# Attention outputs scaled before w_out, one bank for both halves, and a new order of residual and splits at two seams

## What is computed

```python
h = h + 0.5 * rms_norm(f, ffn1_post_g)                       # the residual stream called h3 below
z = rms_norm(h, mix_pre_g) @ w_in                            # "in2"
q_na, k_na, v_na, c_q, c_kv, k_rope = jnp.split(z, split_at, axis=-1)
o_na = neighbourhood_attention(...)                          # 8 heads of 64
o_mla = latent_attention(...)                                # 8 heads of 64
mixed = concatenate([rms_norm(o_na, na_out_norm_g),
                     rms_norm(o_mla, mla_out_norm_g)], -1) @ w_out
h = h + rms_norm(mixed, mix_post_g)                          # the residual stream called h4 below
f = swiglu(rms_norm(h, ffn2_pre_g), ffn2_w_gu, ffn2_w_down)
h = h + 0.5 * rms_norm(f, ffn2_post_g)
```

## Time and profile before

| | us |
|---|---|
| median of 3 runs | 998.67 |
| lowest and highest | 997.17 and 1002.05 |
| the profiled execution | 994.14 |
| its span (first to last instruction) | 992.4 |

### The profile page before, as it was taken

The page is one execution under the profiler, slowest core; times in us unless marked ns, Lnnn a source line. Parts: engine busy times, 40 slices in busy tenths (PEclk is TensorE's granted clock), DMA queues, the critical chain, the costliest instruction groups (busy, mean ns, idle before and its releaser), DMA issues.

```text
span 992.4 us, 13886 instructions
## 1 busy us (share of the span) xinstructions
PE 952.9 (96%) x4548; PEld 786.9 (79%) x4548; DVE 502.7 (51%) x841; ACT 491.2 (49%) x771; POOL 337.3 (34%) x170
## 2 busy tenths in 40 slices
PE   8998979999999999999999999998999989999997
PEld 6876867888878888888878888887878868888886
DVE  5439596554544434343564434337488674334332
ACT  5353935654455454444544454436436464444442
POOL 2410000102434444344444444553512034343442
PEclk9999999999999999999999999999999999999999
DMA  7844454354655566778566566655612246665562
GB/s 232 282 131 147 144 173 141 109 153 142 204 161 181 174 190 190 239 225 242 175 183 190 171 192 188 188 157 161 190 43 86 85 147 194 192 187 175 190 190 81
DMA packets 132768, 169.29 MB, mean 171 GB/s; under 512 B 16707, under 2 KB 88430, under 8 KB 132598
## 3 DMA queue, kind: packets, MB, share of 16 engines
q1 hardware_dynamic: 132566, 168.67, 55.1%
q10 hardware_dynamic: 160, 0.07, 0.0%
HBM read 167.61 MB, written 1.10 MB: 170 GB/s over the span
## 4 chain that ended last, share of the span: by engine, by line
PE 79%; DVE 11%; ACT 5%; issue 3%; DMA 0%; POOL 0%; DVEq 0%; POOLq 0%; ACTq 0%; SPq 0%
PE acc L786 24%; PE acc L788 24%; PE acc L787 24%; PE tp L831 4%; DVE w_lo L1173 4%; ACT w_hi L462 1%; PE sc L916 1%; PE acc L1108 1%; DVE u L1261 1%; ACT junk L468 1%; DVE xt_lo L1556 1%; DVE u L1225 0%; DVE u L1321 0%; DVE h L1546 0%; PE tp L936 0%
## 5 line engine op out<-in xcount | busy, mean ns | idle before, releaser
L462 ACT ACTIVATE w_hi<-w_raw 128x1024 fp32r<-128x1024 f32 x305 | 322.0, 1060 | 376.2 <-PE acc L788 346.0
L1770 POOL TENSOR_TENSOR w_lo<-w_raw,w_hi 128x1024 fp32r<-128x1024 f32 x124 | 302.5, 2440 | 397.0 <-ACT w_hi L462 396.9
L1173 DVE TENSOR_TENSOR w_lo<-w_raw,w_hi 128x1024 fp32r<-128x1024 f32 x181 | 234.8, 1306 | 330.6 <-ACT w_hi L462 328.9
L786 PE MATMUL acc<-w_hi,xt_hi 128*128 128x512 f32 (+1 forms) x880 | 350.0, 398 | 9.5 <-DVE w_lo L1173 6.6
L788 PE MATMUL acc<-w_lo,xt_hi 128*128 128x512 f32 (+1 forms) x880 | 342.9, 390 | 0.0
L787 PE MATMUL acc<-w_hi,xt_lo 128*128 128x512 f32 (+1 forms) x880 | 342.2, 389 | 0.0
L786 PEld LDWEIGHTS acc<-w_hi,xt_hi 128*128 128x128 f32 x880 | 165.3, 188 | 46.6 <-DVE w_lo L1173 9.7
L788 PEld LDWEIGHTS acc<-w_lo,xt_hi 128*128 128x128 f32 x880 | 165.1, 188 | 34.7
L787 PEld LDWEIGHTS acc<-w_hi,xt_lo 128*128 128x128 f32 x880 | 165.5, 188 | 32.0
L786 PE MATMUL acc<-w_hi,hid_hi 128*128 128x512 f32 x264 | 103.2, 391 | 0.0
L788 PE MATMUL acc<-w_lo,hid_hi 128*128 128x512 f32 x264 | 102.8, 389 | 0.0
(11 more groups left out here) (198 smaller groups left out, 781.7 us busy)
## 6 DMA issues: line engine op xcount, KB each, us to landing
w_raw<-in_ffn_w_gu SPq DMA_DIRECT2D x176, 256.0 KB
w_raw<-in_w_in SPq DMA_DIRECT2D x68, 512.0 KB
w_raw<-in_w_ffn_in SPq DMA_DIRECT2D x88, 256.0 KB
w_raw<-in_ffn_w_down SPq DMA_DIRECT2D x44, 512.0 KB
w_raw<-in_w_ffn_out SPq DMA_DIRECT2D x22, 512.0 KB
w_raw<-in_w_rnn_out SPq DMA_DIRECT2D x8, 512.0 KB
w_raw<-in_w_attn_out SPq DMA_DIRECT2D x8, 512.0 KB
w_raw<-in_w_o SPq DMA_DIRECT2D x8, 512.0 KB
```

The costliest lines, as they stand in the source:

```text
L462: act.activation(w_hi[:, b, :], w_raw[:, b, :], ACT.Copy).then_inc(hi_done[b], 1)
L786: pe.matmul(o, hi[:, k, rows], wh, start=first and n == 0, stop=False)
L1173: dve.tensor_tensor(w_lo[:, b, :], w_raw[:, b, :], w_hi[:, b, :].bitcast(F32), ALU.subtract).then_inc(lo_done[b], 1)
L1770: pool.tensor_tensor(w_lo[:, b, :], w_raw[:, b, :], w_hi[:, b, :].bitcast(F32), ALU.subtract).then_inc(lo_done[b], 1)
```

## The change

It has two parts.

1. **w_out.** The outputs of both attentions are now multiplied by their row factors in SBUF (`scale_values`, two instructions of 128x512 on VectorE for each attention) before they are transposed, so that na's and mla's products can be summed in one bank. The groups "top" and "bot" become one pair, "out2"; the drains of top and the adding of bot are gone, and the seam reads the bank directly, as at h3 (`post_squares`, `gained`). To have na's factor in time, its squares move from n = 10 to n = 9 on ScalarE, its mean from n = 12 to n = 10 on VectorE, the scaling stands at n = 11, and the turns move from n = 10 and 11 to n = 12 and 13. GpSimd takes na's power before its second slab of w_out. The turns of mla's output move from after the first slab to after the third.
2. **The seams h3 and h4.** On VectorE the residual is added before the two slabs' low parts are written, and of these one is written before each half of `xt_lo`. On ScalarE the squares of tile 1 stand between the two halves of the split of tile 0.

The core of the diff:

```diff
-MQK_AT, ONA_AT = 4, 10
+MQK_AT, ONA_AT = 4, 12
...
             post_squares("f2", 1, G["f2o"] + 1, S["f2o"] + 21, (0,))
             feed(S["in2"], 2)
-            split_new("h3", 0, mix2_g)
+            split_new("h3", 0, mix2_g, (0,))
             post_squares("f2", 1, G["f2o"] + 1, S["f2o"] + 21, (1,))
+            split_new("h3", 0, mix2_g, (1,))
             feed(S["in2"] + 2, 2)
...
-                if n == ONA_AT:
+                if n == 9:
                     for m in range(MT):
                         wait_drained(act, G["na"], m)
                         square("na", 0, m, o2[:, 0, m, :])
...
+            for c in range(2):
+                post_squares("mix", c, G["out2"] + c, S["out2"] + 5 + 2 * c, (0,))
+            feed(S["f3i"], 2)
+            split_new("h4", 0, f3_g, (0,))
+            for c in range(2):
+                post_squares("mix", c, G["out2"] + c, S["out2"] + 5 + 2 * c, (1,))
+            split_new("h4", 0, f3_g, (1,))
+            feed(S["f3i"] + 2, 2)
+            squares_new("h4", 0)
+            split_new("h4", 1, f3_g)
             squares_new("h4", 1)
...
+            def out2_products(half, c, q, ms=range(MT)):
+
+                s, g = S["out2"] + 4 * half + 2 * c + q, G["out2"] + c
+                wait(pe, lo_done[s % RING], s // RING + 1)
+                slab_products(s, [(0, 4 * half + 2 * q), (1, 4 * half + 2 * q + 1)], XT, W,
+                              acc[g % 2 * 2:g % 2 * 2 + 2], half == 0 and q == 0, half == 1 and q == 1, ms=ms,
+                              done=(acc0_full[g % 2], slab_used[s % RING]))
...
+            last = (S["f2o"] + 10, S["f2o"] + 21)
+            finish("f2", 0, G["f2o"], 1, last, h_new)
+            feed(S["in2"], 1)
+            split_new("h3", 0, mix2_g, (0,))
+            feed(S["in2"] + 1, 1)
+            split_new("h3", 0, mix2_g, (1,))
+            finish("f2", 1, G["f2o"], 1, last, h_new)
+            feed(S["in2"] + 2, 1)
+            split_new("h3", 1, mix2_g, (0,))
+            feed(S["in2"] + 3, 1)
+            split_new("h3", 1, mix2_g, (1,))
...
+            def scale_values(name, which, done):
+
+                dve.wait_ge(rs_done, NTH[name])
+                for m in range(MT):
+                    dve.tensor_scalar(o2[:, which, m, :], o2[:, which, m, :], rs[:, ST[name], m:m + 1], None,
+                                      ALU.mult).then_inc(done, 1)
...
-                if n == ONA_AT + 2:
+                if n == 10:
                     mean_square("na")
+                if n == 11:
+                    scale_values("na", 0, na_scaled)
             drain_values2(1, G["mla"])
+            mean_square("mla")
+            scale_values("mla", 1, mla_scaled)
```

More of the change, by code:

```diff
@@ L678, in _, with split_new @@
             mix2_g = par[:, PAR["mix2_g"]:PAR["mix2_g"] + KT]
-            def split_new(name, m, gain):
-                for half in range(2):
+            def split_new(name, m, gain, halves=range(2)):
+                for half in halves:
                     x = X[name] + 2 * m + half
@@ L747, in _ @@
                 square("mla", 0, m, o2[:, 1, m, :])
+            feed(S["out2"] + 4, 2)
             for k in range(2):
                 split(X["omla"] + k, (4 + 2 * k, 5 + 2 * k), par[:, PAR["mla_g"] - 4:PAR["mla_g"] + 4], xt_hi)
-            feed(S["out2"] + 4, 4)
+            feed(S["out2"] + 6, 2)
             f3_g = par[:, PAR["f3_g"]:PAR["f3_g"] + KT]
[L752 to L762, removed]
+            for c in range(2):
[8 more added lines that the diff above has]
+            split_new("h4", 1, f3_g)
             squares_new("h4", 1)
@@ L1141, in _ @@
                 for c in range(2):
[L1142 to L1143 removed]
                     for q in range(2):
[L1145 to L1146 removed]
                         ready(q)
[L1148 to L1149 removed]
+                        out2_products(1, c, q, (m,))
                         if (m, c, q) == (1, 1, 0):
@@ L1565, in _, with finish @@
             mix2_g = pcol("mix2_g")
-            for m in range(MT):
-                mean_square("f2", m)
-                gained("f2", G["f2o"] + 1, 1, 1, S["f2o"] + 21, (m,))
-                feed(S["in2"] + 2 * m, 2)
-                for g in (G["f2o"], G["f2o"] + 1):
-                    wait_drained(dve, g, m)
-                add_normed("f2", m, h_new, lambda m, c: f[:, m, c * W:(c + 1) * W])
-                split_new("h3", m, mix2_g)
+            def finish(name, m, g, row, last_slabs, done):
+                mean_square(name, m)
+                gained(name, g + 1, 1, row, last_slabs[1], (m,))
+                for c in range(2):
+                    wait_drained(dve, g + c, m)
+                add_normed(name, m, done, lambda m, c: f[:, m, c * W:(c + 1) * W])
+            last = (S["f2o"] + 10, S["f2o"] + 21)
[9 more added lines that the diff above has]
+            split_new("h3", 1, mix2_g, (1,))
             mean_square("h3")
@@ new lines, in _ @@
+            last = (S["out2"] + 5, S["out2"] + 7)
+            gained("mix", G["out2"], 0, 2, last[0], (0,))
+            finish("mix", 0, G["out2"], 2, last, h_new)
+            feed(S["f3i"], 1)
+            split_new("h4", 0, f3_g, (0,))
+            feed(S["f3i"] + 1, 1)
+            split_new("h4", 0, f3_g, (1,))
+            gained("mix", G["out2"], 0, 2, last[0], (1,))
+            finish("mix", 1, G["out2"], 2, last, h_new)
+            feed(S["f3i"] + 2, 1)
+            split_new("h4", 1, f3_g, (0,))
@@ L1745, in statistics3 @@
+            feed(S["f3i"] + 3, 1)
+            split_new("h4", 1, f3_g, (1,))
             def statistics3():
```

57 lines of the change are left out of this document (15 added, 42 removed).

## The result

The changed kernel takes **1016.80 us** (1015.82 to 1017.53, four runs) against 998.94 us for the kernel before; the ratio of the runs is 1.018, with a 95% interval of 1.0162 to 1.0197. The forecast had the sign right and the size wrong: +9.5 us and a range up to 1013, where +17.9 was measured. The profiled execution took 1016.76 us (span 1014.9), the profiled one of before 994.14 (span 992.4).

What follows compares the result with a forecast made beforehand. TensorE bounds the touched stretches, so losses pass on in full. h3 +3.2, attention +3.3, h4 +3.0 and w_out 0 give +9.5 us: 1003.6 profiled, 1008.2 us median, range 1003 to 1013.

Steps and rivals of the forecast that it cites:

- The h3 seam: At h3, first product 2.0 us earlier, but TensorE waits for the third and fourth slabs' low parts: +3.2 us.
- The h4 seam: At h4, same shape as at h3, low parts late, tile 1's turn at 17.2 to 17.6 us: +3.0 us.
- The attention: Squares of na at head 9 and turns at heads 12 and 13: 0.6 + 2.5 + 0.2 = +3.3 us.
- Head 10's exponentials: On ScalarE in the attention, they start at 757.3 instead of 753.84, behind the wait for the drained banks.
- Head 12's turn: On TensorE in the attention, it comes at 762.6 against 762.03, part of the delay made up: +0.6 us.
- the two turns: Turns of na, now at heads 12 and 13, cost 3.2 us, of which 0.7 already fell behind head 12: +2.5.
- Scaling: Two new VectorE instructions of 128x512 for na, 0.3 to 0.6 us each; TensorE's turn of na waits for both.
- The GpSimd collision at head 13: GpSimd's second low part, about 761.8 to 764.2, overlaps VectorE's `nm` of head 13; with the scaling +0.2 us.
- w_out: In w_out, three slabs cover the wait of mla's turns for squares, power and scaling: cost nothing.
- The sum: Both seams and the attention: 3.2 + 3.3 + 3.0 = +9.5 us, median 1008.2; chance 0.65.
- rival C: Clock falls to 1.2 GHz in TensorE's seam idle times: h3 3.3 more, h4 3.8; 1011.5 or 1015.3; chance 0.17.

Runs made afterwards that it cites:

- experiment 8: Changed kernel with two low parts earlier on VectorE at each seam, and na's squares behind head 10's exponentials with mean, scaling and turns one head later: 994.68 us.
- experiment 6: Changed kernel with na's squares on ScalarE behind head 10's exponentials, and mean, scaling and turns one head later: 1010.00 us.
- experiment 5: Changed kernel with useless identity products filling TensorE's five longest waits, 14 and 12 at each seam, 11 at head 10: 1005.46 us.
- Experiment 1: The kernel before, run again unchanged to see each run's clock: 998.05 us, ratio 0.9993.

## Why the prediction was right in its steps and wrong in its size

**The h3 seam.** Counted from the first turn, the forecast had the first product at 3.0, the third at 9.5, tile 1's turn at 10.7, the fourth at 14.9 and tile 1's products at 16.0. With the waits filled and the clock at 1.00 these are 3.0, 9.0, 10.2, 14.3 and 15.6, and the stretch costs +2.6 for +3.2. After, with the clock low, tile 1's products come at 18.0, and more is lost behind them: +6.7. The order and its chain were right, the price of the waits 0.6 high.

**The h4 seam.** Third product at 10.3 to 10.6 forecast, 9.6 measured; tile 1 at 17.2 to 17.6, 16.7 with the waits filled. +3.0 forecast, +2.3 at full clock, +4.8 in the run.

**The attention.** Head 10's exponentials were forecast for 757.3 on the clock of before. They come at 766.85, and all up to there stands 9.76 later, so 757.1. Head 12's turn was forecast for 762.6; with the waits filled it comes at 767.17, less 4.68 of delay, 762.5. Behind it come +2.5, as forecast for the two turns, and the whole is +3.0 for +3.3. What the forecast didn't say is what this price stands for. In experiment 8, whose attention is that of experiment 6, head 13's turn comes 2.3 us earlier than before, since the two turns are gone from heads 10 and 11; they then cost 3.1 us from there on, and +0.8 is left. In the changed kernel ScalarE's stand uses up that lead. So the turns cost what I had put on them, but 2.2 of the 3.0 us come back once the squares stand at head 10 and the turns one head later.

**Scaling.** The two instructions start 0.40 us apart, between my ends of 0.3 and 0.6, where VectorE's 1024 elements of a low part take 1.13 from one to the next. That is less than half of it (0.57), so the rule of the Trainium skill, "VectorE: DVE Perf Modes", section "Mode 2×_2P", is borne out in direction; the 0.3 us estimated by it was 0.1 too low. The GpSimd collision at head 13 did not come in the profile of after, where both engines were late by different amounts. With the waits filled it came where it was forecast: GpSimd's low part runs from 766.09 to 768.44, VectorE's `nm` of head 13 starts in it at 767.26 and takes 1.21 us instead of 0.17, and TensorE's first turn of na waits 0.96 us for the scaled output. All of this lies within the +2.5.

**w_out**: forecast 0, measured 0.0, and no idle time at mla's turns.

**The step that failed is the clock.** The sum reckoned every wait at its length alone and put the lower level behind it at nothing. The waits that I summed to +9.5 measured +7.6 to +7.9 (experiment 5 against the runs and the profile of before). The other 10.2 of the 17.9 us are the lower level, which I had put aside as rival C with a chance of 0.17. In C itself two things were off. First, I counted C for the two seams alone (3.3 and 3.8; the filled run gives 4.1 and 2.4). I had written down that head 10's exponentials come 3.4 us late and that TensorE's turn of head 10 is queued behind them, but then asked only when head 12's turn would come, +0.6. The idle time at head 10, 2.81 us, makes head 12's turn only 0.5 us late, and so stood in my sum with 0.6; yet the clock fell behind it, and it cost 5.1 us, the largest of the three. With it C comes to 3.3 + 3.8 + about 5 above the sum, 1020 us: the right cause, and 3.5 us more than was measured. Second, the chance was too low. What spoke for it stood ahead of the prediction: the profile of before was 4.53 us below its median, and I carried that over as an offset instead of asking what the other executions had that this one had not. Experiment 1 answers it: falls of the clock behind waits of 1.7 to 2.7 us, shorter than the ones that I was adding.

The Trainium skill says it too, in "TensorE: Matmul & The Clock Gate", section "HAM oscillation — how this bites in real kernels": idle gaps of TensorE bring the slow clock back, and each restart is cold. The traces here agree in part: after, the clock fell in or behind four of the five long waits and was already low in the fifth. But the gaps in that section's example are of 3 to 5 us, while here it also fell behind waits of 1.65 to 2.7 us, and behind a wait of 2.7 us in one execution and not in another.

**What settles the cause and what stays open.** Filling the waits gives back 11.3 us and the two reorderings give back 22.1 without a single useless product (10.2 and 21.0 against the kernels before beside them); the stretches of the table, with the early falls ahead of the h3 seam, add up to the whole difference between the profiles in each of these runs, so no further cause is needed for it. How the 17.9 us divide among the parts in a typical run is less sharp than the table, which rests on one profile for each kernel. What decides whether the clock falls behind a given wait, and how long it stays low, stays open.

## What to carry to other kernels

A wait of the engine that bounds the kernel has two prices: its length where it isn't made up later, and the chance of the lower clock behind it, here as much again or more; so list every idle time that a change makes, also the ones that delay nothing; here the clock fell behind waits of 1.65, 1.91, 2.17, 2.69 and 2.72 us in the one profile of experiment 1. Moving a residual ahead of side work helps, provided that the work the next product waits for isn't itself queued behind an instruction that waits for a later stage: the same new order was 1.5 to 2.2 us faster than before at each seam once two low parts stood before the waits instead of behind them. Where a profile stands below the median of its runs, read the clock of the other runs before using the difference as an offset.

## What was not expected of the hardware

- The fall lags. The products behind the wait of 2.69 us at 93.69 ran 1.2 us at full speed first, those at h3 after were slow from the start, and at h4 the level was back at 1.00 in 824 to 826 us while TensorE did nothing at all.
- The same instructions with the same wait fell in one execution and not in another. The kernel before thus has times from 993.95 to 1002.27 us at clocks from 0.999 to 0.989, 6 us for each 0.01.
- A product of two float32 tiles of 128x128 is recorded as two passes and took 0.22 us, twice a turn of the same size (0.11).
